# Gated linear attention spread over the 32 pieces of its last four input panels, heads 0 and 1 first

## The reference

```python
def gla_mixer(u, w_in, w_gk2, b_gk, g_norm, w_out):
    proj = u @ w_in                       # q 512, k 512, v 1024, g 1024, gk_lr 16
    q, k, v, g, gk_lr = jnp.split(proj, [...], axis=-1)
    log_a = log_sigmoid(gk_lr @ w_gk2 + b_gk) / 16
    cum = cumsum(log_a over the chunk)
    q_fwd = qc * exp(cum)
    a_fwd = q_fwd @ (kc * exp(-cum)).T
    a_bwd = (qc * exp(-cum)) @ (kc * exp(cum)).T
    o_intra = where(lower, a_fwd, a_bwd) @ vc
    k_to_end = kc * exp(cum[-1] - cum)
    # over the chunks: o_inter = q_fwd @ S; S = S * exp(cum[-1]) + k_to_end.T @ v
    o = (o_intra + o_inter) * rsqrt(mean(square) + 1e-6) * g_norm
    return (o * silu(g)) @ w_out
```

## Time and profile before

| | us |
|---|---|
| three runs | 2009.07, 2011.65, 2017.13 |
| median | 2011.65 |
| profiled execution | 2010.51 |
| its span | 2008.8 |
| TensorE busy over the span | 1845.5 (92%) |
| VectorE, ScalarE, GpSimd busy | 1176.2, 745.9, 799.3 |
| last projection piece of `gla_in` ends | 176.4 |
| first transpose for the out projection | 279.4 |
| first matmul of the out projection | 285.1 |

### The profile page before, as it was taken

How to read it: one execution, slowest core, us unless ns; L and a number is a source line. 1 busy time by engine, 2 the same in 40 slices (tenths; PEclk the granted TensorE clock), 3 DMA queues, 4 the chain that set the end, 5 groups by cost and what they waited for, 6 DMA issues and landing times.

```text
span 2008.8 us, 25061 instructions
## 1 busy us (share of the span) xinstructions
PE 1845.5 (92%) x9107; PEld 1487.4 (74%) x9107; DVE 1176.2 (59%) x1772; ACT 745.9 (37%) x1166; POOL 799.3 (40%) x577
## 2 busy tenths in 40 slices
PE   4999679999999899989999999988999899989989
PEld 3887457788888767777777888876788777667767
DVE  5643735976776761554487777777388633115562
ACT  2233235222222253545342222324345554445451
POOL 4443004565655344222346656552423243432222
PEclk7998879999999899988999999998999999999899
DMA  8673003555455223211256555541112122222111
GB/s 320 226 256 104 0 22 126 187 180 167 146 168 179 102 84 105 74 63 54 63 185 213 162 170 159 167 147 52 64 63 69 64 66 82 85 83 74 64 53 42
DMA packets 116902, 235.67 MB, mean 117 GB/s; under 512 B 8113, under 2 KB 25393, under 8 KB 115793
## 3 DMA queue, kind: packets, MB, share of 16 engines
q1 hardware_dynamic: 113776, 227.17, 34.4%
q10 hardware_dynamic: 3040, 7.34, 1.1%
HBM read 232.36 MB, written 2.13 MB: 117 GB/s over the span
## 4 chain that ended last, share of the span: by engine, by line
PE 38%; issue 35%; POOL 19%; DVE 6%; ACT 2%; POOLq 0%; DVEq 0%; ACTq 0%
PE bank L216 19%; POOL wsp L2036 18%; PE bank L403 8%; PE bank L1123 2%; PE bank L1164 2%; PE bank L1127 1%; PE bank L1234 1%; PE bank L1218 1%; PE bank L1195 1%; PE bank L1623 1%; PE bank L1399 1%; ACT wsp L179 1%; PE bank L291 1%; DVE fP L1296 0%; DVE hst L1856 0%
## 5 line engine op out<-in xcount | busy, mean ns | idle before, releaser
L2036 POOL TENSOR_TENSOR wsp<-raw,wsp 128x512 fp32r<-128x512 f32 x528 | 786.3, 1521 | 1189.6 <-ACT wsp L179 1189.6
L216 PE MATMUL bank<-xT,wsp 128*128 128x512 f32 x2592 | 607.5, 394 | 7.6 <-POOL wsp L2036 3.9
L216 PEld LDWEIGHTS bank<-xT,wsp 128*128 128x128 f32 x2592 | 488.6, 189 | 119.0 <-issue 10.2
L179 ACT ACTIVATE wsp<-raw 128x2048 fp32r<-128x2048 f32 x132 | 252.1, 1914 | 645.5 <-PE bank L216 294.8
L403 PE MATMUL bank<-wsp,hT 128*128 128x512 f32 x1536 | 369.6, 401 | 20.1 <-DVE hT L505 11.0
L403 PEld LDWEIGHTS bank<-wsp,hT 128*128 128x128 f32 x1536 | 294.0, 192 | 93.0 <-DVE hT L505 11.2
L216 PE MATMUL bank<-wsp,xT 128*128 128x512 f32 x1248 | 295.8, 396 | 4.8 <-DVE tok L1874 2.5
L216 PEld LDWEIGHTS bank<-wsp,xT 128*128 128x128 f32 x1248 | 234.8, 190 | 56.2 <-DVE tok L1874 2.7
L517 DVE TENSOR_TENSOR htmp<-bank,gate 128x512 f32<-128x512 f32 x112 | 76.9, 686 | 56.7 <-PE bank L403 56.7
L505 DVE TENSOR_TENSOR hT<-h,hT 128x512 fp32r<-128x512 f32 x64 | 95.3, 1548 | 15.5 <-ACT hT L466 15.5
L500 DVE TENSOR_TENSOR h<-h 128x512 f32<-128x512 f32 x64 | 56.8, 903 | 80.7 <-ACT h L461 80.4
(11 more groups left out here) (297 smaller groups left out, 2046.1 us busy)
## 6 DMA issues: line engine op xcount, KB each, us to landing
raw<-in_ff_w SPq DMA_DIRECT2D x64, 1024.0 KB, 5.4
ada_ring<-in_w_ada SPq DMA_DIRECT2D x48, 384.0 KB, 3.7
ada_ring<-in_ada_w SPq DMA_DIRECT2D x48, 384.0 KB, 3.8
ring<-in_w_ada SPq DMA_DIRECT2D x64, 256.0 KB, 5.9
raw<-in_odd_w_in SPq DMA_DIRECT2D x16, 1024.0 KB, 5.6
raw<-in_gla_w_in SPq DMA_DIRECT2D x12, 1024.0 KB, 7.5
raw<-in_att_w_in SPq DMA_DIRECT2D x12, 1024.0 KB, 5.1
raw<-in_even_w_in SPq DMA_DIRECT2D x12, 1024.0 KB, 5.1
```

Of the source, the lines that this page charges most:

```text
L179: act.activation(wsp[:, slot, 0], raw[:, slot], ACT.Copy).then_inc(hi_made, 1)
L216: mm = pe.matmul(out_ap, l, r, start=(start and n == 0), stop=(stop and n == 2))
L2036: ins = pool.tensor_tensor(wsp[:, slot, 1, k], raw[:, slot, k], wsp[:, slot, 0, k].bitcast(F32), ALU.subtract)
```

## The change

**The last four panels become 32 pieces** in the order v0, g0, v1, g1 (`GLA_PANEL` swaps two). The low-rank product moves ahead of them. A piece is (tile, half) from `PIECE`, so a panel is (0,0) (1,0) (0,1) (1,1) (2,0) (3,0) (2,1) (3,1), eight pieces, and tiles alternate between two banks only (`GLA_D`, 2 and 3). Between pieces stand the parts of the attention: slot i is piece i and what is written behind it. Heads 0 and 1 go while v0 and g0 pass, heads 2 and 3 while v1 and g1 do. Chunk states come in two parts of four and three.

**The gate** is not one pass on ScalarE: three passes (exp, log, exp) give the sigmoid, and VectorE multiplies it by the bank (`gate`). A piece of a g tile's bank waits for that product.

**Modulation.** VectorE takes tiles 0 to 33 before slot 0 and then two or one in each of slots 0 to 19. The queue has eight tiles behind each of halves 2 to 5 and five behind each of halves 6 to 11. Rows come in slots 28 and 29, the columns after piece 31. The results go to `gg` in place, `tok` keeps the modulation sum; the first transposes wait for the column add.

```diff
+        PIECE = ((0, 0), (1, 0), (0, 1), (1, 1), (2, 0), (3, 0), (2, 1), (3, 1))
+        GLA_S, GLA_D, GLA_O, GLA_KV = 0, 2, 4, 6
+        GLA_PANEL = (0, 1, 2, 4, 3, 5)
...
+            def piece(i):
+                seq, (t, h) = 2 + i // 8, PIECE[i % 8]
+                if h == 0:
+                    before = 4 * (seq - 2) + t - 2
+                    if before < 0:
+                        pe.wait_ge(free, KT + ST)
+                    elif before // 4 % 2 == 0:
+                        pe.wait_ge(free, KT + 2 * ST + before // 8 * 4 + before % 4 + 1)
+                    else:
+                        pe.wait_ge(s["g"], before // 8 * 4 + before % 4 + 1)
...
+            def chunk_states(h, part):
+                if part:
+                    pe.wait_ge(s["state"], 2 * h + 1)
...
+            low_rank()
+            for i in range(4 * 8):
+                piece(i)
+                if i == 1:
+                    gate_logits()
+                for h, at in enumerate((4, 6, 15, 18)):
+                    if i == at:
+                        turned(h)
+                for h, at in enumerate((5, 7, 16, 19)):
+                    if i == at:
+                        scores(h)
+                for h, at in enumerate((10, 13, 24, 27)):
+                    if i in (at, at + 1):
+                        chunk_states(h, i - at)
+                for h, at in enumerate((12, 17, 26, 30)):
+                    if i == at:
+                        output(h)
+                if i == 28:
+                    pe.wait_ge(ada0_used, N0)
+                    pe.wait_ge(s["at"], GLA_H)
+                    pe_modrow(pe, acc0, 2 * D, GLA_S, mod_done)
+                if i == 29:
+                    pe.wait_ge(mod_made, 2)
+                    pe_modrow(pe, acc0, D, GLA_S, mod_done)
+            pe.wait_ge(mod_made, 3)
+            pe_modcols(pe, acc0, range(24, 40), GLA_S, mod_done, ST * KT)
...
+                achain(act, act.activation(gg[:, t, c], ps, ACT.Exp, scale=-1.0))
+                achain(act, act.activation(gg[:, t, c], gg[:, t, c], ACT.Ln, bias=1.0))
+                act.activation(gg[:, t, c], gg[:, t, c], ACT.Exp, scale=-1.0).then_inc(s["sg"], 1)
...
+            for i in range(4 * 8):
+                for h, at in enumerate((1, 1, 6, 8)):
+                    if i == at:
+                        softplus(h)
+                for h, at in enumerate((2, 3, 13, 16)):
+                    if i == at:
+                        exps(h)
+                for h, at in enumerate((4, 6, 15, 18)):
+                    if i == at:
+                        keys(h)
+                for h, at in enumerate((13, 18, 27, 31)):
+                    if i == at:
+                        squares(h)
+                evac(i)
+                if i % 8 in (5, 7):
+                    act_high(act, base["gla_in"] // 2 + 3 + i // 8, i % 8 // 6)
...
+            modulation(range(0, 34))
+            n = 34
+            for i in range(4 * 8):
+                if i < 20:
+                    modulation(range(n, n + 2 - i % 2))
+                    n += 2 - i % 2
...
+                for h, at in enumerate((3, 5, 13, 17)):
+                    if i == at:
+                        scaled(h)
+                for h, at in enumerate((5, 7, 16, 19)):
+                    if i == at:
+                        taken(h)
+                for h, at in enumerate((10, 13, 24, 27)):
+                    if i in (at, at + 1):
+                        states(h, i - at)
+                for g, at in enumerate((11, 12, 15, 16, 27, 28, 31)):
+                    if i == at:
+                        gate(g)
+                if i == 16:
+                    written(0, range(ST))
...
-                p, h = divmod(j, 2)
+                p, h = GLA_PANEL[j // 2], j % 2
                 sp_half(sp, j, h, w[:, HK * h:HK * h + HK, p * COLS:p * COLS + COLS])
-                for g in range(6 * j - 10, 6 * j - 4 if j < 11 else 8 * KT):
+                for g in range(g, g + (8 if j < 6 else 5)):
                     ada0_tile(g)
+                g += 1
```

More of the change, by code:

```diff
@@ new lines, in gla_pe @@
+            free = TS["in_gla_in"]["bank_free"]
+            def piece(i):
[8 more added lines that the diff above has]
+                        pe.wait_ge(s["g"], before // 8 * 4 + before % 4 + 1)
+                for k in range(HK):
+                    if t == 0:
+                        low_ready(pe, base["gla_in"] + 2 * seq + h, k)
+                    mm = pe_tile(pe, bank[GLA_D + t % 2][:, :], h, k, HK * h + k, t, "N", h == 0 and k == 0, h == 1 and k == HK - 1)
+                if t == 3:
+                    mm.then_inc(w_used, 1)
+                elif h == 1:
+                    mm.then_inc(tile_done, 1)
@@ new lines, in low_rank, with gate_logits @@
+            def low_rank():
+                pe.wait_ge(lohi_made, 2)
+                pe.wait_ge(free, KT + ST)
+                for k in range(KT):
+                    for q, (a, b) in enumerate([(0, 0), (0, 1), (1, 0)]):
+                        mm = pe.matmul(bank[GLA_S][:, :], lohi[:, b, k, :], xT[:, a, k, :], start=(k == 0 and q == 0),
+                                       stop=(k == KT - 1 and q == 2))
+                mm.then_inc(gkT_done, 1)
+            def gate_logits():
+                pe.wait_ge(gk2_ld, 16)
+                pe.wait_ge(s["gkT"], 1)
+                pe.wait_ge(free, KT + 2 * ST)
+                for h in range(GLA_H):
+                    pe.matmul(bank[4 + h][:, :], wgk2[:, h * P:h * P + P], gkT[0:GLA_R, :], start=True, stop=True)\
+                      .then_inc(s["pre"], 1)
@@ L1013, in taken, with states @@
                 dve.sem_inc(s["at"], 1)
-            def states(h):
-                dve.wait_ge(s["kv"], h + 1)
-                if h:
+            def states(h, part):
+                dve.wait_ge(s["kv"], 2 * h + part + 1)
+                if h and not part:
                     dve.wait_ge(s["o"], h)
-                for n in range(1, NC):
+                for n in range(4 * part + 1, min(4 * part + 5, NC)):
                     kv = gla_kv(n - 1)
@@ L1056, in gla_dve @@
+            dve.wait_ge(s["out"], 8)
+            dve.sem_inc(TS["mid_gla_out"]["tok_ready"], 1)
+            written(2, range(3))
+            gate(7)
+            written(2, range(3, 4))
+            written(3, range(ST))
             dve.wait_ge(s["out"], 4 * GLA_H)
             dve.sem_inc(TS["mid_gla_out"]["tok_ready"], 1)
+            dve.wait_ge(mod_done, 4)
+            dve.tensor_tensor(modcol[:, 24:40], bank[GLA_S][:, 24:40], col("b_ada", 24, 16), ALU.add).then_inc(mod_made, 1)
         PAIRS = HEADS // 2
```

270 lines of the change are left out of this document (117 added, 153 removed).

## The result

| | median us | runs |
|---|---|---|
| before | 2010.99 | 2009.07 to 2017.13 (4) |
| after | 2029.41 | 2027.7 to 2032.37 (4) |

The change makes the kernel slower: the ratio is 1.0088, with a 95% interval from 1.0063 to 1.0113. That is outside the predicted range of 2000 to 2024 us. The span of the profiled execution is 2030.6 us, against 2008.8 before.

What follows compares the result with a forecast made beforehand. Bound: gated attention, TensorE busy 73.3 of 105.6 us at clock 0.75. Start 89.8, work 136.6, long waits 31.1, short 15.3, clock 4.2 end piece 31 at 277.0; out projection at 286.5 gives 2012.0 us, range 2000 to 2024.

Steps and rivals of the forecast that it cites:

- both long waits: TensorE waits ahead of head 1's second states part and piece 17, behind late modulation tiles: 15.8 and 15.3 us.
- The VectorE gaps: Sign in the trace: two gaps of 15 to 20 us ended by a ring DMA, before scaled(2) and taken(2).
- The clock: TensorE returns at 1.2 GHz after each long wait, costing 2.1 us each, 4.2 together.
- since TensorE has been busy for long by then: Ground for starting the out-projection transposes at 283.0 us, between 282.2 and columns at half clock, 284.3.
- Rival C: TensorE drops to 1.2 GHz in short waits too, lower clock lasts longer, tiles take 8.1 us: 2026 us; chance 0.14.
- Short waits, in order: TensorE's smaller waits between pieces, for VectorE's tiles, passes, states and gate products: 15.3 us in all.
- Turn 1: TensorE's transposes of head 1 wait for VectorE's taken(0): 2.2 us.
- tile 44 and tile 49: Tile 44, behind half 8, makes states(0) wait 3.1 us; their second part waits 1.9; tile 49 not named.
- TensorE leaves panel 1 at 89.8 us: Start of the sum: TensorE finishes panel 1 at 89.8 us, released by ScalarE's split of the next half.
- Work at full clock: TensorE's work from 89.8 us to the end of piece 31: 136.6 us, with pieces at 2.72 us each.
- A: Rival: every slot holds, tiles come before VectorE wants them: 1961 us; chance 0.05.
- B: Rival: one long wait is covered, its half and tile leaving the queue early: 1994 us; chance 0.07.

Runs made afterwards that it cites:

- e6: e2 with the one-column modulation products behind piece 30 instead of 31, their bias and three head 3 writes ahead of the last gate product: 1994.91 us, ratio 0.9907.
- e8: e2 plus gate products first in VectorE's slots, e6's early columns, and head 0's scores ahead of four passes of head 1: 1983.2 us, ratio 0.9854.
- e13: Changed kernel with unused products filling five of TensorE's waits: median 2027.91 us, ratio 1.0067; profiled execution 2020.8 us.
- e12: e9 with the tiles of halves 6 and 7 also ahead of their raw copies in the queue: 2022.26 us, ratio 1.0037.
- e3: Changed kernel with six tiles behind half 2 and ten behind half 3 instead of eight and eight: 2029.33 us, ratio 1.0088.
- e4: Changed kernel without modulation tiles 34 to 63, the 30 tiles of the slots, transfer and sum: 1984.76 us, ratio 0.9868.
- e7: Changed kernel with GpSimd's split of weight half 6 cut to 8 of 512 columns: 2027.0 us, ratio 1.0068.
- e9: Changed kernel with GpSimd's splits of weight halves 5 and 6 cut to 8 of 512 columns: 2027.8 us, ratio 1.0074.
- e2: Changed kernel with the tiles of all six halves 6 to 11 ahead of the raw copy in SyncE's queue: 1994.7 us, ratio 0.9926.
- e10: e8 with the 32 one-column products in four groups of eight between the matmuls of piece 31: 1983.23 us, ratio 0.985.
- e11: e10 without modulation tiles in slots 1 to 3 (two each in slot 0 and slots 4 to 17): 1987.38 us, ratio 0.9871.
- e1: Changed kernel with the tiles of halves 10 and 11 ahead of their raw copies in SyncE's queue: 2004.7 us, ratio 0.9967.

## Why the prediction was wrong

**Right: both long waits.** Place, cause and size: 15.8 and 15.3 predicted, 14.87 and 14.05 measured. The VectorE gaps that led to them were 23.0 and 15.0 us, where 15 to 20 had been named as the sign. The chain of the second, as this profile has it (GpSimd, SyncE's queue, VectorE):

```profile
205.05 4.92 POOL L2133 TENSOR_TENSOR wsp<-raw,wsp 128x512 fp32r<-128x512 f32 x4 [22.36 <-ACT wsp L179]
```

```profile
210.00 0.38 SPq L161 DMA_DIRECT2D raw<-in_gla_w_in  x1
```

```profile
215.94 0.75 DVE L591 SCALAR_TENSOR_TENSOR tok<-ring,csil,tok 128x512 f32<-128x512 f32 x1 [14.97 <-DMA ring<-in_w_ada]
```

From raw to tile it is 5.9 us in both where 6.3 and 6.4 stood in the sum. The split took 4.92 us beside a VectorE that waits, as in the earlier trace rows; the 7.44 of a busy one did not come up. The rule of the Trainium skill on the shared port (page SBUF — State Buffer, section SBUF: two separate sides) agrees with that. The same section of the Trainium skill also says that VectorE's instructions with two inputs in SBUF contend with GpSimd's reads, which the passes of 1.67 to 1.76 us bear out. I weighed the rule only for what it does to GpSimd, where it cost nothing, and not for what it does to VectorE, where it did.

**Failed: "The clock".** The term was 4.2 us, 2.1 behind each long wait; 13.1 were lost. Behind the two long waits alone it was 1.8 and 3.0. The other 8.3 lie where the prediction had none: behind the gate logits (3.4), behind the wait of 4.86 us ahead of head 1's transposes (1.6), and behind those of 4.15 and 2.82 us (3.4). Another 3.0 fell on the transposes for the out projection. These were counted at full clock, 3.5 us, and the columns ahead of them nearly so, "since TensorE has been busy for long by then". That sentence counted busy time; in e6 and e8 the clock falls behind 32 one-column products in a row although TensorE does not wait there. The step that failed is thus the price of the clock outside the two long waits: put at nothing, 8.3 us up to piece 31 and 3.0 in the transposes. Rival C had this mechanism in part, and its 2026 us was the nearest number; it was given 0.14 on the ground that 2.15 us did not lower the clock and 5.61 did. Between those two no row shown there decided, and five of the seven short waits lay between them. But the trace of the kernel before did hold more, table by stretch:

```profile
188.40:195.20 6.80, 6.80 (x33) 6.80 (x33) 4.69 (x6) 5.27 (x11) 0.00 (x0) 0.50 0.00 0
...
205.60:221.30 15.70, 8.56 (x38) 7.70 (x38) 15.09 (x24) 6.58 (x13) 0.00 (x0) 0.50 0.00 0
```

The first stretch follows the gate logits, ahead of which TensorE had waited 0.73 us; the columns of the earlier trace rows are in it, at the lower clock while TensorE is busy throughout. The second follows waits of 1.65 and 2.45 us. Both the fall behind a wait near 2.5 us and the fall without one could be read before the change. C was not right throughout: the clock fell behind the waits of 4.86, 4.15 and 2.82 us (5.0 lost), but not behind those of 1.58, 1.08 and 2.92, C had nothing for the gate logits or the transposes, and its number leans on slower tiles that did not come. What the clock is worth in time is less sure than what it takes in the profile: e13 gave back 4 us of 9.

**Failed in size: "Short waits, in order".** The sum, 17.9 against 15.3, hides larger errors that partly cancel. Turn 1 was given 2.2 and took 4.86, because VectorE's passes were taken at 0.69 us although GpSimd's split falls beside them; the front gave tile 36 as used at 105 us and it was used near 111, since six tiles took 8.37 us instead of 4.8 (0.8 each in the prediction) and raw half 6 left at 102.7. e12 takes both out and gives 2022.3 us, inside the range, but with the low parts of two halves left out. The waits for tile 44 and tile 49 came up as VectorE's, and reached TensorE as 1.08 and 4.15 us (3.1 and 1.9 predicted).

**Failed: the start.** "TensorE leaves panel 1 at 89.8 us" took panel 1 as unchanged. Eight tiles stand behind half 2 before half 3 can leave the queue. It left at 66.3 us (58.9 in the kernel before), and the low-rank products started at 92.4. What this error cost is not shown: e3 moved the half by 2.3 us only, and the time did not change.

**Work at full clock** was 3.4 us too small: a piece was taken as 2.72 us from one eviction interval, while five of them in a row in the changed kernel took 13.9, 2.78 each, and one with other work ahead and behind 2.9.

**Rivals.** A (1961) fell: e4 shows it out of reach without any tile. B fell, since both waits are there. C differed from the forecast mainly in the term on the clock, and that was the forecast's wrong one.

## What to carry over

When an engine's waits are shortened into many small ones, ask of each, and of each stretch of small matmuls, what the granted clock is behind it. Price it like the wait itself: here the two long waits were predicted to 2.2 us in 31, and the clock missed by 9. Where the same wait or stretch comes out both ways, price it as a range, and don't judge 1 or 2 us by one profile. In a queue that serves two masters, put the small transfers ahead of the large one that has to wait for a buffer: that was worth 35 us here, more than anything else. And before taking an instruction's duration from a quiet stretch, look at what will run beside it in its new place; two causes that cover each other show nothing until both are taken out.

## What the runs showed of the hardware

- VectorE's passes with both inputs in SBUF (128x512) took 0.69 us alone and 1.67 to 1.76 beside a GpSimd split; the split took 6.5 us beside them and 4.9 beside an idle VectorE (changed kernel; e7, e9 and e12 for the passes without a split).
- TensorE's clock fell to its lower level (1.2 GHz) behind waits of 2.45 us (e4; in the kernel before, too, behind one of 2.45 with one of 1.65 ahead of it), 2.82 and 4.15 us, but not behind one of 2.15 nor one of 2.92 at 271.0 us in the changed kernel (a piece of 3.04), where the same wait in e2 was followed by a piece of 4.61. What decides between these was not found.
- It fell with no wait at all behind 32 one-column products in a row (e8, piece of 5.47 us instead of 3.03). In groups of eight between the matmuls of piece 31 they ran at full clock in e10 and not in e11 (0.50 from 249.8 us).
- It fell behind the gate logits of 16 rows (0.57 from 105.4 to 113.4 us in the changed kernel), but not in every profile: in e1, e6, e7, e10 and e12 they were followed by full clock.
